# Expert loop: next rows ahead of a weight piece; HGRN gate block split by token halves; head norm weights folded into a later copy

## What is computed

```python
# layer 0, mixer
g_qkv, g_z, g_b, g_a, h_q, h_f, h_i, h_g = split_cols(h @ w_in, EVEN_SPLITS)
o_a = gated_delta_rule(q, k, v, beta, g)                         # 4 heads of 128, 8 chunks of 64 tokens
o_a = rms_norm(o_a, gdn_norm_w) * silu(split_heads(g_z, 4))      # first gate: g_z
o_b = hgrn2_recurrence(silu(h_q), 1 - f_gate, h_i, log(f_gate))  # 4 heads of 128, 8 chunks of 64 tokens
o_b = rms_norm(o_b, hgrn_norm_w) * silu(split_heads(h_g, 4))     # HGRN gate: h_g
x = x + concatenate([o_a, o_b], -1) @ w_out
# hgrn2, one chunk
o = (q_i * exp(b_i)) @ state + attn @ i_i
state = state * exp(b_last) + (k_i * exp(b_last - b_i)).T @ i_i
# both layers, experts: top 2 of 16 for each token
gate, up = split(x @ w_gate_up[e]);  y = (silu(gate) * up * gates) @ w_down[e]
```

## Time and profile before

| | |
|---|---|
| median of 3 runs | 1240.08 us (1239.59 to 1240.46) |
| profiled execution | 1240.35 us, of it 1238.2 us from first to last instruction |
| PE busy | 1131.0 us (91%) |
| DVE, ACT, POOL busy | 700.4, 595.6, 417.7 us |
| mean granted TensorE clock | 0.949 of full |

### The profile page before, as it was taken

The page is one execution under the profiler, slowest core; times in us unless marked ns, Lnnn a source line. Parts: engine busy times, 40 slices in busy tenths (PEclk is TensorE's granted clock), DMA queues, the critical chain, the costliest instruction groups (busy, mean ns, idle before and its releaser), DMA issues.

```text
span 1238.2 us, 19697 instructions
## 1 busy us (share of the span) xinstructions
PE 1131.0 (91%) x7097; PEld 926.7 (75%) x7097; DVE 700.4 (57%) x990; ACT 595.6 (48%) x845; POOL 417.7 (34%) x350
## 2 busy tenths in 40 slices
PE   6998999999999699998399999999999996999990
PEld 4786888777788578886378888888888885778870
DVE  4434434379653799997515542452432137999974
ACT  5545234232333388888232324233342234888871
POOL 4342311210124234333434243543334332344432
PEclk8989999999989799999599999999999997999995
DMA  9232311102107499996633232332222363999945
GB/s 256 64 79 47 67 39 36 52 28 74 55 18 230 141 353 368 368 366 216 241 104 92 77 94 68 95 109 60 94 69 85 103 195 127 337 368 369 371 166 212
DMA packets 89284, 194.88 MB, mean 157 GB/s; under 512 B 19901, under 2 KB 21241, under 8 KB 88186
## 3 DMA queue, kind: packets, MB, share of 16 engines
q1 hardware_dynamic: 67562, 160.00, 39.0%
q10 hardware_dynamic: 11856, 17.07, 4.0%
q0 software_dynamic: 9792, 16.80, 3.7%
HBM read 189.63 MB, written 23.07 MB: 172 GB/s over the span
## 4 chain that ended last, share of the span: by engine, by line
PE 80%; DVE 9%; ACT 5%; DMA 2%; issue 2%; POOL 1%; POOLq 0%; SPq 0%; DVEq 0%; ACTq 0%
PE ps L631 23%; PE ps L633 22%; PE ps L632 22%; PE ps L2136 2%; PE ps L2339 2%; ACT wh L1203 1%; PE ps L1991 1%; PE ps L2023 1%; DMA arena<-y 1%; PE ps L2309 1%; DMA arena<-hs,slot_rows 1%; DVE arena L1388 1%; DVE x L1369 1%; DVE x L1370 1%; PE ps L1967 1%
## 5 line engine op out<-in xcount | busy, mean ns | idle before, releaser
L794 POOL TENSOR_TENSOR wl<-raw,wh 128x1024 fp32r<-128x1024 f32 x100 | 243.0, 2439 | 466.1 <-ACT wh L960 465.6
L631 PE MATMUL ps<-wh,hT_hi 128*128 128x512 f32 x864 | 349.4, 404 | 10.1 <-ACT wh L1203 4.5
L633 PE MATMUL ps<-wh,hT_lo 128*128 128x512 f32 x864 | 339.7, 393 | 0.0
L632 PE MATMUL ps<-wl,hT_hi 128*128 128x512 f32 x864 | 338.8, 392 | 0.0
L960 ACT ACTIVATE wh<-raw 128x1024 fp32r<-128x1024 f32 x116 | 122.7, 1068 | 225.5 <-PE ps L633 206.3
L631 PEld LDWEIGHTS ps<-wh,hT_hi 128*128 128x128 f32 x864 | 163.7, 189 | 51.0 <-issue 12.8
L633 PEld LDWEIGHTS ps<-wh,hT_lo 128*128 128x128 f32 x864 | 163.5, 189 | 35.7
L632 PEld LDWEIGHTS ps<-wl,hT_hi 128*128 128x128 f32 x864 | 163.8, 190 | 31.5
L631 PE MATMUL ps<-hT_hi,wh 128*128 128x512 f32 x288 | 117.0, 406 | 8.2 <-ACT arena L1112 5.3
L1807 DVE TENSOR_TENSOR wl<-arena,wh 128x1024 fp32r<-128x1024 f32 x96 | 117.4, 1225 | 10.1 <-ACT wh L1203 3.2
L1807 DVE TENSOR_TENSOR wl<-raw,wh 128x1024 fp32r<-128x1024 f32 x92 | 112.3, 1225 | 13.0 <-ACT wh L960 4.6
(11 more groups left out here) (315 smaller groups left out, 1542.1 us busy)
## 6 DMA issues: line engine op xcount, KB each, us to landing
raw<-in_moe_w_gate_up_dram SPq DMA_DIRECT2D x64, 512.0 KB
arena<-in_moe_w_gate_up_dram SPq DMA_DIRECT2D x64, 512.0 KB, 7.7
raw<-in_odd_w_in_dram SPq DMA_DIRECT2D x48, 512.0 KB
raw<-in_even_w_in_dram SPq DMA_DIRECT2D x32, 512.0 KB
arena<-in_moe_w_down_dram SPq DMA_DIRECT2D x32, 512.0 KB, 8.4
raw<-in_moe_w_down_dram SPq DMA_DIRECT2D x32, 512.0 KB
arena<-y ACTq DMA_DIRECT2D x8, 1024.0 KB, 8.2
raw<-in_odd_w_out_dram SPq DMA_DIRECT2D x16, 512.0 KB
```

The lines of the kernel that those rows point to most:

```text
L631: nc.tensor.matmul(dst, lh, rh, start=first, stop=False)
L632: nc.tensor.matmul(dst, lh, rl, start=False, stop=False)
L633: return nc.tensor.matmul(dst, ll, rh, start=False, stop=last)
L794: pool.tensor_tensor(columns_of(i, wl[:, i % NSPL, :, :]), raw_columns(i), columns_of(i, wh[:, i % NSPL, :, :]).bitcast(F32), ALU.subtract ...
```

## The change

Four things are changed; names are those of the diff.

1. In the expert loop, `xT_hi` on ACT stands ahead of `hi_in(7)`, and `xT_lo` on DVE ahead of `lo_in(7)`.
2. The order of layer 0's mixer is written anew. All gates of block 6 are read by ACT after the fourth level, into four buffers `zt` instead of two; the products by DVE (`zmul`) stand between the first chunks. Block 7 is made by token halves: tiles 0 and 1 of all four pieces between the last levels, tiles 2 and 3 between chunks 0 to 3. `splits_at` and `dve_splits_at` say which pieces are split at these steps. Rows of block 8 stand between chunks 4 to 7.
3. PE makes the state products of two chunks (`states_of`) in one go, in alternation between the upper and lower 64 partitions, and leaves out those of the last chunk of both scans, which nothing reads. DVE's sum then also waits for the chunk's output tile.
4. The head norm weights are one column each (`head_w`), applied as the scale of ACT's high copy and in DVE's low part of `yT`; the DVE product L1641 goes. The squares of the delta-rule output are summed by ACT per head (four ACT instructions of 128 columns for one of 512), without DVE's reduction.

```diff
-    return {0: [i + 3] if db != MOE_AT[0] else [], NT - 1: [i + 4, i + 5, i + 6]}.get(t, [])
+    return {0: [i + 3] if db not in (8, MOE_AT[0]) else [], NT - 1: [i + 4, i + 5, i + 6]}.get(t, [])
+
+
+def splits_at(step):
+
+    k = step[0]
+    if k == "rows":
+        return ahead_of_rows(*step[1:3]) if len(step) == 3 or 0 in step[3] else []
+    if k == "part" and step[1] == 7:
+        if step[3][0] == 0:
+            return [first_piece(7) + 3] if step[2] == 0 else []
+        return [first_piece(8) + step[2]]
...
+def states_of(c):
+
+    return {0: (0, 1), 2: (2, 3), 4: (4, 5), 6: (6,)}.get(c, ())
...
-        if n < 2:
-            s.append(("oscale", 0, (2 * n, 2 * n + 1)))
-        if n == 2:
-            s.append(("piece", 6, 3))
-        if n in (2, 3):
-            s += [("evac_gate", 6, 2 * n - 4), ("evac_gate", 6, 2 * n - 3)]
-        if n < 2:
+        if n < 3:
             s.append(("piece", 6, n + 1))
-        if n > 2:
-            s.append(("piece", 7, n - 3))
-    s += [("hstate",), ("piece", 7, 3)]
-    for T in range(NT + 1):
-        if T < NT:
-            s.append(("hscan", 2 * T))
-        if T > 0:
-            s.append(("onorm", 1, (T - 1,)))
-        if T < NT:
-            s.append(("hscan", 2 * T + 1))
-        if T > 0:
-            s += [("oscale", 1, (T - 1,)), ("evac_gate", 7, T - 1)]
-        if T > 1:
-            s.append(("yT", 0, 0, (T - 2,)))
-        if T > 2:
-            s.append(("rows", 8, T - 3))
-    s += [("yT", 0, 0, (NT - 1,)), ("rows", 8, 2), ("rows", 8, 3), ("evac", 8)]
+        if n == 3:
+            s += [("evac_gate", 6, t) for t in range(NT)] + [("oscale", 0, (0, 1)), part(7, 0, 0, 1), part(7, 1, 0, 1)]
+        if n == 4:
+            s += [("oscale", 0, (2, 3)), part(7, 2, 0, 1)]
+    s += [part(7, 3, 0, 1), ("hstate",), ("zmul", 0)]
+    s += [("hscan", 0), part(7, 0, 2, 3), ("zmul", 1), ("hscan", 1), part(7, 1, 2, 3), ("zmul", 2), ("hscan", 2), ("onorm", 1, (0,))]
+    s += [part(7, 2, 2, 3), ("zmul", 3), ("hscan", 3), ("oscale", 1, (0,)), ("evac_gate", 7, 0), part(7, 3, 2, 3)]
+    s += [("yT", 0, 0, (0,)), ("hscan", 4), ("onorm", 1, (1,)), ("rows", 8, 0), ("oscale", 1, (1,)), ("evac_gate", 7, 1)]
+    s += [("hscan", 5), ("yT", 0, 0, (1,)), ("rows", 8, 1, (0, 1)), ("hscan", 6), ("onorm", 1, (2,)), ("rows", 8, 1, (2, 3))]
+    s += [("hscan", 7), ("oscale", 1, (2,)), ("evac_gate", 7, 2), ("onorm", 1, (3,)), ("yT", 0, 0, (2,)), ("rows", 8, 2)]
+    s += [("oscale", 1, (3,)), ("evac_gate", 7, 3), ("yT", 0, 0, (3,)), ("rows", 8, 3), ("evac", 8)]
...
-                        A(act.activation(H[:, 4 * g:4 * g + 4, cols(T)], v3(tile(name), 4), ACT.Copy), s_("hT_hi_made"))
+                        scale = head_w[:, g:g + 1] if l == 0 else 1.0
+                        A(act.activation(H[:, 4 * g:4 * g + 4, cols(T)], v3(tile(name), 4), ACT.Copy, scale=scale), s_("hT_hi_made"))
...
-                        hi_in(7)
                         if not last:
                             xT_hi(l, it * 2 + (par + 2), par)
+                        hi_in(7)
...
             def hscan(c):
+                if c == NC - 1:
+                    return
                 D(tt(v3(Stmp[:, :], 4), v3(S[:, :], 4), bc_h(HB[:, :, CH * c + CH - 1]), ALU.mult))
                 tile_is_ready(dve, ("hs", c))
+                tile_is_ready(dve, ("ho", c))
...
-                        D(tt(v3(z, 4), v3(z, 4), bc_m(wgt[:, :]), ALU.mult))
                         D(tt(y, y, z, ALU.mult), s_("z_used"))
...
                         gated(E + 1, 1 - par)
+                        if not last:
+                            xT_lo(l, it * 2 + (par + 2), par)
                         lo_in(b + 7, it)
                         if not last:
-                            xT_lo(l, it * 2 + (par + 2), par)
                             lo_in(b + 8, it)
...
-                t = open_tile(("hs", c))
+                made = states_of(c)
+                t = [open_tile(("hs", m)) for m in made]
                 for h in range(NH):
-                    ins = mm(t[:, cols(h)], KDT[r, T, cols(h)], HI[r, T, cols(h)], start=True, stop=True)
-                done(ins)
+                    for n, m in enumerate(made):
+                        ins = mm(t[n][:, cols(h)], KDT[half(m % 2), T, cols(h)], HI[half(m % 2), T, cols(h)], start=True, stop=True)
+                        if h == NH - 1:
+                            done(ins)
```

More of the change, by code:

```diff
@@ L79, in ahead_of_rows, with dve_splits_at @@
     i = first_piece(db)
-    return {0: [i + 3] if db != MOE_AT[0] else [], NT - 1: [i + 4, i + 5, i + 6]}.get(t, [])
+    return {0: [i + 3] if db not in (8, MOE_AT[0]) else [], NT - 1: [i + 4, i + 5, i + 6]}.get(t, [])
[7 more added lines that the diff above has]
+        return [first_piece(8) + step[2]]
+    if k == "piece" or k == "part" and step[3][0] == 0:
+        return [first_piece(step[1]) + step[2] + 3]
+    return []
+def dve_splits_at(step):
+    k = step[0]
+    if k == "part" and step[1] == 7:
+        at = splits_at(step) if step[3][0] > 0 else {0: [first_piece(7) + 2], 1: [first_piece(7) + 3]}.get(step[2], [])
+    elif k == "piece" or k == "part" and step[3][0] == 0:
+        at = [first_piece(step[1]) + step[2] + 2]
+    else:
+        at = []
+    return [i for i in at if i in DVE_LO]
 def raw_slot(i):
@@ L268, in side_tiles @@
         c = step[1]
-        return [(("sv", c), "dve"), (("so", c), "act"), (("ss", c, 0), "dve"), (("ss", c, 1), "dve")]
+        return [(("sv", c), "dve"), (("so", c), "act")] + [(("ss", c, n), "dve") for n in range(2 if c < NC - 1 else 0)]
     if k == "hdiag":
@@ L276, in side_tiles @@
     if k == "hscan":
-        return [(("ho", step[1]), "act"), (("hs", step[1]), "dve")]
+        c = step[1]
+        return [(("ho", c), "act")] + [(("hs", m), "dve") for m in states_of(c)]
     if k == "score":
@@ L743, in _ @@
                   (dtb, a["gdn_dt_bias"].broadcast_to([P, 4])), (alog, a["gdn_a_log"].broadcast_to([P, 4])),
-                  (gnw[:, :], a["gdn_norm_w"].broadcast_to([P, P])), (hnw[:, :], a["hgrn_norm_w"].broadcast_to([P, P])),
+                  (head_w[:, 0:1], a["gdn_norm_w"].rearrange("a p -> p a")), (head_w[:, 1:2], a["hgrn_norm_w"].rearrange("a p -> p a")),
                   (wba_raw, a["even_w_in"][0].rearrange("(p k) c -> p k c", k=KD)[:, :, 2048:2056])]
-            for dst, src in small_ones:
-                sp.dma_start(dst, src).then_inc(s_("consts_loaded"), 16)
+            with nc.allow_non_contiguous_dma(reason="one value of a head's norm weight per partition"):
+                for dst, src in small_ones:
+                    sp.dma_start(dst, src).then_inc(s_("consts_loaded"), 16)
             def moe_loads(l):
@@ L917, in _ @@
             for step in SCHEDULE:
-                if step[0] == "piece" or step[0] == "part" and step[3][0] == 0:
-                    lo(first_piece(step[1]) + step[2] + 3)
-                elif step[0] == "rows":
-                    for i in ahead_of_rows(step[1], step[2]):
+                if step[0] in ("piece", "part", "rows"):
+                    for i in splits_at(step):
                         lo(i)
@@ L1088, in onorm @@
                 for T in Ts:
[L1089 to L1092 removed]
+                    y = Y0[:, T, 512 * w:512 * w + 512]
+                    if w == 1:
+                        if T >= 2:
+                            act.wait_ge(s_("sq_reduced"), T - 1)
+                        A(act.activation(onsq[:, T % 2, :], y, ACT.Square), s_("o_sq"))
+                        continue
+                    for h in range(NH):
+                        A(act.activation(onsq[:, T % 2, cols(h)], y[:, cols(h)], ACT.Square, accum_out=oss[:, 4 * T + h:4 * T + h + 1]),
+                          s_("o_sq"))
             def hstate():
@@ L1271, in _ @@
                             act.dma_start(dst, src).then_inc(s_("ret_consts"), 16)
-                elif k == "rows":
-                    for i in ahead_of_rows(step[1], step[2]):
+                elif k in ("piece", "part", "rows"):
+                    for i in splits_at(step):
                         hi(i)
-                elif k == "piece" or k == "part" and step[3][0] == 0:
-                    hi(first_piece(step[1]) + step[2] + 3)
                 elif k == "ba":
@@ L1905, in _ @@
                     hgrn(step)
-                elif k == "piece" or k == "part" and step[3][0] == 0:
-                    i = first_piece(step[1]) + step[2] + 2
-                    if i in DVE_LO:
+                elif k in ("piece", "part"):
+                    for i in dve_splits_at(step):
                         lo(i)
@@ L2045, in hT_ready, with rows @@
                     tile_is_read(pe, last + (t, 1))
-            def rows(db, t):
+            def rows(db, t, kps=(0, 1, 2, 3)):
                 hT_ready(db, t)
                 pe.wait_ge(dense_read[evac_engine(db - 1)], evac_count(db - 1, t))
-                for kp in range(4):
+                for kp in kps:
```

(2 more changed lines are left out.)

46 lines of the change are left out of this document (26 added, 20 removed).

## The result

The changed kernel takes 1229.09 us, median of 4 runs (1227.33 to 1230.59), against 1240.27 for the kernel before beside it (4 runs). The direction was right and the size was not. The profiled execution took 1230.59 us (span 1228.5).

What follows compares the result with a forecast made beforehand. PE, busy 91%, bounds the kernel through waits, half clock and removable work. Loop 4.3 plus mixer 2.5 (13.0 - 10.5) minus clock 3.4 saves 3.4 us from 1240.35: 1236.95, stated as 1237.0, range 1232.5 to 1241.0.

Steps and rivals of the forecast that it cites:

- Expert loop, 4.3 us: Expert loop: moving xT_lo ahead of one piece shortens PE's wait before L631, saving 0.165 us 26 times, 4.3 us.
- Saving: 0.55 - 0.38 = 0.165 us: Expert loop, per expert: the 0.55 us from transposes to the next L631 falls to the last pair's 0.38.
- State products, 3.7 us: Layer 0's mixer: two chunks' products together take 1.28 for 2.16 us, three times, and chunk 7's 1.08 goes.
- The figure by the Trainium skill: State products: matmuls on different row groups run side by side, eight take 1.08 us, giving 4.3 instead of 3.7.
- Chunks' waits and the clock between them, 3.3 and 6.8 us: Layer 0's mixer: 3.3 us of waits at levels and chunks and 6.8 us lost to half clock both go.
- The 0.8 for restarts of the dense run: Mixer: splitting block 7 and one rows step into halves restarts the dense run eight times, about 0.1 us each.
- New waits, 10.5 us: New mixer order: waits of 0.6 at hstate, 0.1 and 0.8 at chunks 2 and 4, 2.4 at yT(2), 2.3, 2.0, 2.3 at rows.
- The walk: Mixer: stepping through the new order with the old durations to find what is late, together 10.5 us.
- The clock at the new waits, 3.4 us: Mixer's three places of new waits: the clock falls at the middle and one other, 3.4 us lost.
- the 5.8 that the prediction names for three falls: Upper bound of clock loss at the mixer's new waits: three falls, with transposes at half clock in the middle.
- rival B: Mixer: clock falls at all three new waits and once at chunk 4 or hstate, 5.8 + 1.7; 1240.8 to 1239; chance 0.22.

Runs made afterwards that it cites:

- covered tail: Changed kernel with GpSimd's low part of piece 34 held off, plus layer 0's mixer tail reordered, rows of block 8 cut as cover after yT: 1215.97 us, ratio 0.9795 to before.

## Why the prediction was wrong, point by point

1. **Expert loop, 4.3 us: the step that failed.** "Saving: 0.55 - 0.38 = 0.165 us" took the last pair in the earlier trace rows for a place without a wait, because it "has no next rows to make". It has: in the trace of before DVE makes rows there too, up to 571.47, and PE starts at 571.53.

```profile
570.19 1.28 DVE L1799 TENSOR_TENSOR hT_lo<-ps,hT_hi 128x512 fp32r<-128x512 f32 x2
```

   The 0.38 held a smaller wait, and because the profile prints 0.38 us as the length of the two transposes, a distance of 0.38 looked like none. With the move it is 0.13 (566.79 to 566.92). That it was L1799 that PE awaited there, ACT's move alone shows: its L1799 runs to 585.98, PE again starts 0.06 us behind it, and the trace names it.

```profile
586.04 0.50 PE L631 MATMUL ps<-wh,hT_hi 128*128 128x512 f32 x1 [1.14 <-DVE hT_lo L1799]
```

   Without a wait the distance is 0.14, so the term is 0.41 us and not 0.165, and 26 times that is 10.7. With the loop's change alone an expert takes 9.38 us for 9.79, just these 0.41. Between the changed kernel's loops with and without the new order there are 12.5: 0.5 more come from the two last pairs, 0.7 from the pairs behind the loops' starts, where the old order waits 0.52 and 0.56 us if the clock has stayed up, and some 0.6 are spread thin and not located. The trace of before had a row that comes near this floor: eight such transposes of the rows stand 0.82 us from the next matmul (489.15 to 489.97), which makes 0.2 for two. That the wait belonged to xT_lo and not to ACT's piece was right, and so was that DVE would let the gain through; the transfers took up to 1.9 us of it in layer 1.

2. **State products, 3.7 us: under-sized.** Measured 3 x 1.08 + 1.08 = 4.3. The figure by the Trainium skill ("TensorE: Matmul & The Clock Gate", "Packing small matmuls: row/col tiling"), which stood beside the sum, was the better one. The row that I took instead gives 0.64 for four products, and the eight measured take 1.09, so the second four add 0.45: doubling 0.64 counted twice a part of 0.19 that stands in a group once. What that part is, no run shows.

3. **Chunks' waits and the clock between them, 3.3 and 6.8 us: right.** No wait at the levels' products or at chunks 0 to 3, and the clock at 1.00 from 300 to 326.5. The 0.8 for restarts of the dense run was near, too: the 288 dense matmuls of the stretch take 67.95 us before, 0.4 of it by the clock, and 68.51 in the covered tail, all at full clock, so 1.0.

4. **New waits, 10.5 us: right in sum, by luck in part.** Measured 0.58 at hstate, 1.43, 0.18, 2.29, 2.37, 1.69 and 2.07: 10.6. The one ahead of yT(0) was missing, and those at chunk 4 and at two rows were taken too long. The missing one comes from DVE and GpSimd taking turns. The walk used durations of operations that ran alone, though the trace of before had the collision, in the delta-rule scan: an operation of 0.69 us took 2.25 and ended 0.54 us behind GpSimd's, and at 218.83 another took 1.46 and ended 0.54 behind.

```profile
195.93 2.39 POOL L794 TENSOR_TENSOR wl<-raw,wh 128x1024 fp32r<-128x1024 f32 x1 [2.99 <-ACT wh L960]
```

```profile
196.61 2.25 DVE L1525 TENSOR_TENSOR arena<-arena,small 128x512 f32<-128x512 f32 x1
```

5. **The clock at the new waits, 3.4 us: too small.** It fell at all three places in each of three profiles (the changed kernel's two, and the one with GpSimd held off), and at two of them with the mixer's change alone. In the first: 1.5 us (4.52 for 12 dense matmuls that take 3.01), 1.6 and 0.8 (7.37 for 5.74, and transposes of 1.81 for 1.04), and 1.7 as half of the 3.4 us at 0.50: 5.6 us, near the 5.8 that the prediction names for three falls. So the count of falls was wrong and their price right. The three falls are rival B's; the fourth that it adds, at chunk 4 or hstate, did not come, and its time, 1239 to 1241, did not because the loop gave so much more.

In all: with 12.5 for the loops, 4.3 for the products and 5.6 for the clock, the same sum gives 12.5 + 13.6 - 10.6 - 5.6 = 9.9 us, 1230.4, beside the 1230.59 of the profiled execution. That it comes so near is partly luck, for two differences of about 1.1 us cancel. Between these two profiles the loops give 13.6 and not 12.5: the clock at their starts adds 2.6, and layer 1's late rows take 1.5. And the mixer loses 3.8 and not 2.6. There the waits and the clock are as counted; what is short is work: products less restarts should give 3.5 us, and what is left of the stretch without waits and half clock is 102.8 us before and 100.4 after, 2.4 less. I have not traced the rest to an instruction.

## What to carry to other kernels

The floor of a step is the distance between starts at a place where every operand is known to be early, or that of a longer run of the same instruction divided; a place that merely looks freer, or the duration printed, can hide the wait that one wants to price. Where a step stands on two engines, price each half by itself: here DVE's half alone gave all of the gain, and ACT's alone cost 31 us. When a list is written anew to hide one chain, walk the next chain with the same care: here the new waits of the tail and the clock behind them, 14 us, cost as much as the scan gained, and six to twelve dense matmuls between each yT and its rows, with the gate of one token group moved ahead of the last chunk, gave them back. And look in the trace for an operation that takes several times its usual length: it tells of a collision that durations from elsewhere will miss.
